# Feed-forward chunks of 512 columns instead of 256, units in another order, and the conditioning sums of the first block on VectorE alone

## The reference

```
x = x + 0.5 * mx[2] * swiglu(modulate(rmsnorm(x), mx[0], mx[1]), ffn1_w1, ffn1_w3, ffn1_w2)   # both streams
y = y + 0.5 * mc[2] * swiglu(modulate(rmsnorm(y), mc[0], mc[1]), ffn1_w1, ffn1_w3, ffn1_w2)
...   # one input projection, a gated linear recurrence and a gated long convolution, one output projection
x = x + 0.5 * mx[8] * swiglu(modulate(rmsnorm(x), mx[6], mx[7]), ffn2_w1, ffn2_w3, ffn2_w2)   # latent only
out = rmsnorm(x)
```

## Time and profile before

| | us |
|---|---|
| median of the runs (three) | 3586.87 |
| span of the profiled execution | 3581.1 |
| what the median has beyond that span | 5.8 |
| PE busy | 3255.1 (91% of the span) |
| PEld busy | 2870.1 (80%) |
| DVE busy | 2369.0 (66%) |
| ACT busy | 1321.6 (37%) |
| POOL busy | 557.4 (16%) |

### The profile page before, as it was taken

One profiled execution on the slowest core, in us unless ns is written; L12 is line 12 of the kernel. 1 busy time (PEld: TensorE's weight loads), 2 busy tenths in 40 slices (PEclk: granted clock), 3 DMA queues, 4 the chain that ended last, 5 costly groups with the idle time before them and its releaser, 6 DMA issues.

```text
span 3581.1 us, 54986 instructions
## 1 busy us (share of the span) xinstructions
PE 3255.1 (91%) x19595; PEld 2870.1 (80%) x19595; DVE 2369.0 (66%) x3018; ACT 1321.6 (37%) x1658; POOL 557.4 (16%) x343
## 2 busy tenths in 40 slices
PE   4576988889999999999998899998999899999998
PEld 2445766667777778888887888888999899999998
DVE  5977788877766763443446766766555666666666
ACT  4333433322222222222223776665334443443434
POOL 2764444410000000000000333333000000000000
PEclk7666988889999999999999999999999999999999
DMA  4664545466566643333232444445444455555554
GB/s 171 216 216 162 158 159 164 154 201 203 181 225 219 205 155 95 95 93 95 94 94 82 124 148 133 125 139 156 151 149 159 153 182 181 182 181 182 182 181 135
DMA packets 394040, 562.30 MB, mean 157 GB/s; under 512 B 17699, under 2 KB 304956, under 8 KB 393088
## 3 DMA queue, kind: packets, MB, share of 16 engines
q1 hardware_dynamic: 388896, 547.11, 48.3%
q0 software_dynamic: 1888, 8.19, 0.7%
q10 hardware_dynamic: 3200, 6.29, 0.5%
HBM read 553.14 MB, written 8.39 MB: 157 GB/s over the span
## 4 chain that ended last, share of the span: by engine, by line
PE 70%; DVE 14%; issue 10%; POOL 2%; ACT 2%; DMA 1%; SPq 0%; DVEq 0%; POOLq 0%; ACTq 0%
PE bank L390 22%; PE bank L392 21%; PE bank L391 21%; DVE states L570 3%; DVE w_lo L380 2%; PE bank L589 1%; DVE ada_raw L570 1%; PE bank L1011 1%; DVE lk L1632 1%; PE bank L1153 1%; PE bank L1164 1%; DVE xn L446 1%; POOL ctot L863 1%; POOL csum L861 1%; DVE sq_sum L420 1%
## 5 line engine op out<-in xcount | busy, mean ns | idle before, releaser
L380 DVE TENSOR_TENSOR w_lo<-raw,w_hi 128x1024 fp32r<-128x1024 f32 x736 | 954.6, 1301 | 851.0 <-ACT w_hi L375 846.5
L375 ACT ACTIVATE w_hi<-raw 128x1024 fp32r<-128x1024 f32 x736 | 775.2, 1057 | 1398.9 <-PE bank L392 1377.2
L390 PE MATMUL bank<-h_hi,w_hi 128*128 128x512 f32 (+1 forms) x2816 | 954.5, 339 | 21.9 <-DVE h_lo L458 19.4
L392 PE MATMUL bank<-h_hi,w_lo 128*128 128x512 f32 (+1 forms) x2816 | 954.4, 339 | 0.0
L391 PE MATMUL bank<-h_lo,w_hi 128*128 128x512 f32 (+1 forms) x2816 | 954.2, 339 | 0.0
L390 PEld LDWEIGHTS bank<-h_hi,w_hi 128*128 128x128 f32 x2816 | 532.5, 189 | 85.4 <-issue 16.0
L391 PEld LDWEIGHTS bank<-h_lo,w_hi 128*128 128x128 f32 x2816 | 532.3, 189 | 62.2
L392 PEld LDWEIGHTS bank<-h_hi,w_lo 128*128 128x128 f32 x2816 | 532.2, 189 | 62.2
L390 PE MATMUL bank<-g_hi,w_hi 128*128 128x512 f32 (+1 forms) x1408 | 492.6, 350 | 88.7 <-DVE y_res L734 83.7
L391 PE MATMUL bank<-g_lo,w_hi 128*128 128x512 f32 (+1 forms) x1408 | 484.0, 344 | 0.0
L392 PE MATMUL bank<-g_hi,w_lo 128*128 128x512 f32 (+1 forms) x1408 | 483.0, 343 | 0.0
(11 more groups left out here) (237 smaller groups left out, 3862.7 us busy)
## 6 DMA issues: line engine op xcount, KB each, us to landing
raw<-in_ffn_w_dram SPq DMA_DIRECT2D x528, 512.0 KB, 3.7
ada_raw<-in_ada_w_dram SPq DMA_DIRECT2D x192, 512.0 KB, 4.7
raw<-in_w_in_dram SPq DMA_DIRECT2D x176, 512.0 KB, 3.7
ada_wide<-in_ada_w_dram SPq DMA_DIRECT2D x96, 512.0 KB, 4.4
raw<-in_w_out_dram SPq DMA_DIRECT2D x32, 512.0 KB, 3.4
spec<-spec_spill POOLq DMA_DIRECT2D x8, 768.0 KB, 7.5
spec_spill<-spec_out ACTq DMA_DIRECT2D x4, 1280.0 KB, 9.1
xin<-in_x_dram SPq DMA_DIRECT2D x1, 2048.0 KB, 12.4
```

What stands on the lines that cost most here:

```text
L375: nc.scalar.activation(w_hi[un.slot(j)][:], raw[un.slot(j)][:], ACT.Copy).then_inc(hi_done, 1)
L380: nc.vector.tensor_tensor(w_lo[un.slot(j)][:], raw[un.slot(j)][:], w_hi[un.slot(j)][:].bitcast(F32), ALU.subtract).then_inc(lo_done, 1)
L390: nc.tensor.matmul(o, w_hi[slot][:, c0:c0 + P], hi, start=start, stop=False, skip_group_check=True)
L392: return nc.tensor.matmul(o, w_lo[slot][:, c0:c0 + P], hi, start=False, stop=stop, skip_group_check=True)
```

## The change

`CHUNK` becomes 512, so there are 11 chunks, each with eight units of w1, eight of w3 and eight of w2. The up work of a chunk is done in two halves ("sub") of 256 columns. The loop body has 24 units in this order: w1 of the next chunk's first half (0 to 3), all down units of this chunk (4 to 11), w3 of the first half (12 to 15), w1 of the second half (16 to 19), w3 of the second half (20 to 23). A w2 unit now covers 512 rows by 256 columns (two output blocks) where it covered 256 rows by 512 columns (four). A block d is summed over twelve matmuls, and DVE adds each block once for 512 hidden columns. `silu`, product and rest write and read the same buffers, which lie in `sq2` and `xn2`.

The conditioning loops become four iterations with one half for both streams, four with two halves each for the latent stream, and two with none. In the first kind DVE makes both sums, with two instructions on each tile, one tile in each of the units 0 to 15; the parts of ACT and POOL go. In the second kind two tiles are taken per unit, in the units 0 to 7 and 11 to 18. `ada_total` stands in unit 18 in the first kind and in units 10 and 21 in the second.

```diff
-CHUNK = 256
+CHUNK = 512
+FBLK = CHUNK // P
-ADA_LATENT = 8
+ADA_LATENT = 4
+        g1 = [sq[0], sq[1], xn[0], xn[1]]
+        g2 = [g[:, 0:SEQ] for g in g1]
...
-            return w[bass.ds(chunk * CHUNK, CHUNK), q * 512:(q + 1) * 512].rearrange("(f p) c -> p f c", p=P)
+            return w[bass.ds(chunk * CHUNK, CHUNK), q * 256:(q + 1) * 256].rearrange("(f p) c -> p f c", p=P)
...
+        def ada_steps(j, ada):
+            if ada == 2:
+                return [(0, j)] if 0 <= j < KB else []
+            if ada == 1:
+                if 0 <= j < 8:
+                    return [(0, 2 * j), (0, 2 * j + 1)]
+                if 11 <= j < 19:
+                    return [(1, 2 * (j - 11)), (1, 2 * (j - 11) + 1)]
+            return []
+        ADA_SUM_AT = {2: {18: 0}, 1: {10: 0, 21: 1}, 0: {}}
+        ADA_TAKE_AT = {2: {19: 0}, 1: {11: 0, 22: 1}, 0: {}}
...
+        def ada_step(ve, ada, it, n, m):
+            ada_landed(ve, ada, it, n, m)
+            src = ada_raw[m % RING][:]
+            if m == 0:
+                ve.wait_ge(ada_pe, ada_half(ada, it, n) + (0 if n else 1))
+            for t, total in enumerate(ada_tiles(ada, n)):
+                done = (ada_x, ada_c)[t]
+                if m == 0:
+                    nc.vector.tensor_scalar(total, src, silu_c[:, m, t:t + 1], None, ALU.mult).then_inc(done, 1)
+                else:
+                    ve.wait_ge(done, ada_done(ada, it, n, m))
+                    nc.vector.scalar_tensor_tensor(out=total, in0=src, scalar=silu_c[:, m, t:t + 1],
+                                                   in1=total, op0=ALU.mult, op1=ALU.add).then_inc(done, 1)
...
             def body(un, c, ada, it):
-                for j in range(12):
-                    if j < 8:
-                        up(un, j, c)
+                for j in range(24):
+                    if j < 4:
+                        up(un, j, j, 0, 0, c + 1)
+                    elif j < 12:
+                        down(un, j, j - 4, c)
                     else:
-                        down(un, j, j - 8, c)
+                        up(un, j, j % 4, 0 if 16 <= j < 20 else 1, 0 if j < 16 else 1, c + 1)
...
-            with po.Fori(0, ADA_BOTH) as it:
-                for m in range(1, KB):
-                    ada_gpsimd(po, ada_sum[0], ada_prod[(m - 1) % 2], it * KB + (WIDE + ADA_FIRST_H * ADA_EW + m + 1),
-                               it * (KB - 1) + (3 + ADA_FIRST_H * (ADA_EW - 1) + m - 1))
```

More of the change, by code:

```diff
@@ L50 @@
 U_FFN1 = 0
-U_CTX = U_FFN1 + 12 * N_CHUNK
+U_CTX = U_FFN1 + 24 * N_CHUNK
 U_HG = U_CTX + 12 * PAIRS
@@ L517, in ffn_sync @@
                 sy.wait_ge(ada_pe, 1 + ADA_FIRST_H)
-            ffn_loops(sy, base, body, loops, before)
-            un = Units(base + 8 + 12 * (N_CHUNK - 1))
-            for j in range(4):
+            ffn_loops(sy, base, body, loops)
+            un = Units(base + 16 + 24 * (N_CHUNK - 1))
+            for j in range(8):
                 load_unit(sy, un, j, row_src(w2, N_CHUNK - 1, j))
         ada_w = i["ada_w"][0]
-        def ada_at(j):
-            return range(2 * j, 2 * j + 2) if 0 <= j < 8 else ()
@@ L660, in ffn_pe, with ffn_act, silu @@
-            for j in range(4):
+            un = Units(base + 16 + 24 * (N_CHUNK - 1))
+            for j in range(8):
                 down(un, j, j, N_CHUNK - 1)
-        def ffn_act(ac, s, base, sil, g, g_hi, ntok, loops, norm, res):
-            def silu(un, j, c):
+        def ffn_act(ac, s, base, g, g_hi, ntok, loops, norm, res):
+            def silu(un, j, sub, c):
                 ac.wait_ge(w_used, used(un, j))
@@ L699, in ffn_act, with ghi @@
-            ffn_loops(ac, base, body, loops)
-            un = Units(base + 8 + 12 * (N_CHUNK - 1))
-            for j in range(4):
+                        ac.wait_ge(s["glo"], c * FBLK + (2 * sub + b + 1 - FBLK))
+                    nc.scalar.activation(g[2 * sub + b], up_bank(b, ntok), ACT.Silu).then_inc(s["silu"], 1)
+            def ghi(sub, c):
+                for b in range(2 * sub, 2 * sub + 2):
+                    ac.wait_ge(s["gmul"], c * FBLK + (b + 1))
+                    nc.scalar.activation(g_hi[b][:], g[b], ACT.Copy).then_inc(s["ghi"], 1)
@@ new lines, in step, with body @@
+            def step(un, j, at, c):
+                round_unit(ac, un, j + AHEAD)
+                if j in (at[0], at[2]):
+                    silu(un, j, at.index(j) // 2, c)
+                if j in (at[1], at[3]):
+                    ghi(at.index(j) // 2, c)
+            un = Units(base)
+            for j in range(16):
+                step(un, j, SUB_FIRST, 0)
+            def body(un, c, ada, it):
+                for j in range(24):
+                    if j == 12:
+                        ac.wait_ge(w_used, used(un, 11))
+                    step(un, j, SUB_LOOP, c + 1)
@@ L723, in add, with glo @@
+            def glo(sub, c):
+                for b in range(2 * sub, 2 * sub + 2):
+                    ve.wait_ge(s["ghi"], c * FBLK + (b + 1))
+                    nc.vector.tensor_tensor(g_lo[b][:], g[b], g_hi[b][:].bitcast(F32), ALU.subtract).then_inc(s["glo"], 1)
             def add(un, j, jj, c, norm=None):
```

200 lines of the change are left out of this document (87 added, 113 removed).

## The result

| | before | after |
|---|---|---|
| median of the runs, us | 3588.8 (4 runs, 3582.4 to 3591.2) | **3472.6** (4 runs, 3469.0 to 3478.4) |
| ratio | | 0.9678, 95% interval 0.9667 to 0.9689 |
| span of the profiled execution | 3581.1 | 3476.6 |
| DVE busy | 2369.0 | 2116.1 |
| POOL busy | 557.4 | 371.8 |

The forecast was 3473.6. The profiled execution of after was its slowest (3478.4), so its span shows 104.5 us less; two later profiled executions of the same kernel have spans of 3468.2 and 3470.0.

A forecast was written before the change was run, and what follows sets the result against it. PE's own work was taken as the bound, apart from stops in FFN1's first twelve iterations. 98.2 + 6.0 + 10.1 - 1.0 = 113.3 us off 3586.9 gave 3473.6 us, range for 8 in 10 3463 to 3506.

The forecast's parts named there:

- FFN1's loop, 98.2: FFN1's loop stretch: PE's stops and slow restarts go, 1538.5 us becomes 1440.3, 98.2 us less.
- its end, 6.0: End of FFN1: time beyond PE's units falls from 11.1 to 5.1 us, 6.0 less.
- two conditioning instructions a down unit at 2.66 us each, 21 us an iteration: FFN1's first loop: if DVE's conditioning stayed at its duration beside GpSimd, 21 us per iteration, 83 in all, lost.
- The slack of 1.4: FFN1's unit 4: DVE adds block 0 at 7.0 us, PE wants its bank at 8.4; slack grows afterwards.
- The clock behind ada_total: FFN1, after ada_total with both streams: 1.6 us of slow clock as now, or 0; up to 6.5 gain, not summed.
- FFN2, 10.1 less 1.0 in the tail: FFN2: small waits for a bank go, 21 x 0.48 = 10.1 us less; weight rests in its tail cost 1 more.
- The 5.8 us between span and median: Whole kernel: the median of the runs lies 5.8 us above the profiled span, added to reach the forecast.
- A: FFN1's first loop: DVE still comes late, giving up to 83 us back, 3557 us, halfway 3515; chance 0.12.
- B: FFN1's second loop: tiles come late, 34 us in four iterations if 2 us per pair, 3508 us; chance 0.08.
- C: Loop turns: engines stop because the body is not at hand, 9.4 us a turn, 188 in all, 3662 us; chance 0.04.

The follow-up runs named there:

- chunk_only: The kernel after, but ctx sums of the first four iterations again as ScalarE product and GpSimd addition, with one product buffer; 3474.3 us, ratio 0.9679 to before.
- extra_rest: The kernel after with the weight rest computed twice on VectorE in each of eight down units of the first four iterations; 3495.2 us, ratio 0.9735 to before.
- again: The kernel after, unchanged, in another set of executions; 3474.3 us, ratio 0.9687 to before.
- after_b: The kernel after, unchanged, in a further set of executions; 3471.7 us, ratio 0.9672 to before.

## Why the prediction was right

**FFN1's loop, 98.2, and its end, 6.0.** Together 104.2 were forecast, 105.1 and 106.7 came. The iterations were forecast at 139, 137.4 and 133.8 and are 138.6, 137.4 and 133.9. From the loops' end to the last sum are 49.5 us; PE's units behind it, 44.6, and 5.1 make 49.7.

**The reason given for it was too narrow.** As the cost of GpSimd's presence I priced two conditioning instructions a down unit at 2.66 us each, 21 us an iteration. No kernel here runs that: where GpSimd adds, VectorE makes one sum a unit and not two. It also held the slow duration throughout, while chunk_only has GpSimd busy in 149 of 559 us, one conditioning instruction of 3.50 us and the next, alone, of 1.27. The cost there was no time that can be measured, though it took the distance to a stop down to 0.45 us. So the gain doesn't rest on GpSimd's leaving, as I had it: moving the context's sums to VectorE is worth 52 us at 256 columns and nothing that can be measured at 512.

**The slack of 1.4** shows in the kernel after itself as 1.6. Unit 4 of the first iteration, the add that frees block 0's bank and PE's first matmul for block 3:

```profile
468.41 0.47 DVE L766 SCALAR_TENSOR_TENSOR y_res<-bank,gate,y_res 128x256 f32<-128x256 f32 x1
470.48 0.40 PE L389 MATMUL bank<-g_hi,w_hi 128*128 128x512 f32 x1
```

It grows to 2.7 in the later down units, as forecast, and extra_rest gave 1.7 for it by another way.

**The clock behind ada_total** was put at 1.6 in each of four iterations, 6.4 in all, with 0 as the other end. It was between: 3.2 and 1.6 in two iterations of the first profile, 1.6 in two of the second. The reason that I gave for the other end, the long stop ahead of it, isn't the cause: the fall came without a stop, and went when the row of small matmuls was halved.

**FFN2, 10.1 less 1.0 in the tail.** The step was right in mechanism: the waits went, and in the fast cadence an iteration takes 68.36 (683.60 / 10) where 68.4 was forecast. Net it gave 7.6 in place of 9.1, since what lies beside the iterations grew by 1.8 and not by 0.5. The cadence is what the step had missed: I took the fast one from the earlier trace rows and did not see that two stretches of before are slow. In the first profile it cost 6.6 us and hid nearly the whole gain.

**The 5.8 us between span and median** were read as something beside the span. They were the distance between one execution and the median: the time of a run is 1.6 to 2.0 above its own span in every later profile. Taking the difference off the median gave the right size all the same. Why before's other runs are up to 17 us longer than the profiled one no profile here shows; their mean granted clock is lower, 0.940 in the longest run against 0.945 in the shortest.

**That the sum met the median to 1.0 us is in part luck.** The change of the medians was 116.2, 113.9 and 117.3 us in the three sets (the first, again, after_b) against 113.3, FFN2 gave less than its term in all three profiles of the kernel after, FFN1 a little more, and the median from which I subtracted, of three runs, lies 2 below that of the four.

**Rivals.** A (VectorE late) and B (tiles late) would show as waits of PE in the loop; there are none. For B, VectorE notes no wait on a landing tile there either. C (a stop at each turn) likewise: the instruction queue moved 44 packets in the whole execution in place of 30, and PE waited at no turn. The rule of the Trainium skill, Runtime: NRT & Kernel Launch, section "Instruction fetch mechanics", by which it could have come, doesn't show with bodies twice as long either. The same section gives PE room for 2048 instructions, though, and a body of 576 matmuls with their weight loads is some 1200: read so, the rule asks for no stop here, and these traces can't test it.

## What to carry to other kernels

Work that is shed onto an engine beside the critical one should be priced by how much of it falls between two points at which the critical engine waits, not by its sum: the same sums, spread over twice the matmuls, stopped PE nowhere, and made cheaper in their old place they still stopped it 4.0 us an iteration. Slowdown by a neighbour counts only for the time in which the neighbour runs (3.50 us beside GpSimd, 1.27 in the next unit), and it can be seen how near it comes to a stop by the distance from the add to the matmul that needs its bank. And where a gain of a few us is looked for, count the instructions of a wait-free window in two executions of the same kernel first.

## What the hardware showed that was not expected

- Rows of 256-column matmuls run 0.1187 or 0.1200 us apart at the same granted clock (1.00), with no wait recorded; one execution kept the slow one for over 700 us of FFN2, while in three kernels with small waits it came for about 30 us at a time, begun 173.4 us apart (once 104.1). The 512-column ones are 0.232 apart in both.
- The granted clock fell to the 1.2 GHz level behind 32 one-column matmuls (3.6 us), in two to four of four places, and never behind 16.
- A stop of 4.5 us an iteration, split into six waits, cost no slow restart; one of 2.86 us was followed by 3 us at 0.43.
